# One transformer trunk layer on one core: the first modulation's weight slices issued by ScalarE, its vectors made as columns, and VectorE's order at the beginning and between the halves

## What is computed

```python
c_act = jax.nn.silu(c)
mod = (c_act @ w_ada[l] + b_ada[l])[:, None, :]
sh1, sc1, g1, sh2, sc2, g2 = jnp.split(mod, 6, axis=-1)
h = rms_norm(x, norm1_g[l]) * (1.0 + sc1) + sh1
proj = h @ w_in[l]          # attention q, k, v | conformer | short gated convolution | pooling
...
x = x + g1 * mix
h = rms_norm(x, norm2_g[l]) * (1.0 + sc2) + sh2
x = x + g2 * (jnp.square(jax.nn.relu(h @ w_ff1[l])) @ w_ff2[l])
```

## Time and profile before

| | |
|---|---|
| median of 3 runs | 2392.0 us (2390.57 to 2394.45) |
| the profiled execution | 2397.45 us |
| its span | 2395.2 us, mean granted clock of TensorE 0.978 |
| TensorE busy | 2304.6 us, 96% |
| VectorE busy | 1750.8 us, 73% |
| ScalarE busy | 983.4 us, 41% |
| GpSimd busy | 342.5 us, 14% |
| DMA | 177.67 MB, mean 74 GB/s |

### The profile page before, as it was taken

The page is one execution under the profiler, slowest core; times in us unless marked ns, Lnnn a source line. Parts: engine busy times, 40 slices in busy tenths (PEclk is TensorE's granted clock), DMA queues, the critical chain, the costliest instruction groups (busy, mean ns, idle before and its releaser), DMA issues.

```text
span 2395.2 us, 31303 instructions
## 1 busy us (share of the span) xinstructions
PE 2304.6 (96%) x11618; PEld 1943.3 (81%) x11618; DVE 1750.8 (73%) x2654; ACT 983.4 (41%) x1607; POOL 342.5 (14%) x245
## 2 busy tenths in 40 slices
PE   5999899987989999999999999999999999999999
PEld 3987897666888888888888888888888888888887
DVE  5548796888989786777676776767687676767676
ACT  4532555458888754423232323233433222223231
POOL 0343044822345440000000000000000000000000
PEclk9999999988999989999999999999999999999999
DMA  7441533120000034111111111136201111111112
GB/s 259 154 154 53 162 115 129 58 92 23 14 14 23 10 106 132 36 53 53 53 53 53 53 45 60 35 105 210 79 18 53 53 53 53 53 53 53 53 53 88
DMA packets 108278, 177.67 MB, mean 74 GB/s; under 512 B 5512, under 2 KB 77468, under 8 KB 107164
## 3 DMA queue, kind: packets, MB, share of 16 engines
q1 hardware_dynamic: 108188, 176.45, 22.3%
HBM read 152.84 MB, written 23.59 MB: 74 GB/s over the span
## 4 chain that ended last, share of the span: by engine, by line
PE 83%; DVE 9%; DMA 3%; ACT 3%; issue 2%; POOL 1%; SPq 1%; DVEq 0%; ACTq 0%; POOLq 0%
PE ps L2470 10%; PE ps L2468 10%; PE ps L2469 10%; PE ps L2506 7%; PE ps L2505 7%; PE ps L2507 7%; PE ps L2171 5%; PE ps L2172 5%; PE ps L2173 5%; PE ps L2358 3%; PE ps L2343 2%; PE ps L2413 2%; PE ps L2414 2%; PE ps L2415 2%; PE ps L2378 2%; DVE ps L1592 2%
## 5 line engine op out<-in xcount | busy, mean ns | idle before, releaser
L1958 DVE TENSOR_TENSOR sb_x_new<-sb_x_new,ps 128x512 f32<-128x512 f32 x512 | 347.3, 684 | 107.4 <-PE ps L2470 101.9
L2468 PE MATMUL ps<-sb_w_hi,sb_u_hi 128*128 128x512 f32 x1024 | 398.3, 389 | 0.0
L2469 PE MATMUL ps<-sb_w_lo,sb_u_hi 128*128 128x512 f32 x1024 | 398.3, 389 | 0.0
L2470 PE MATMUL ps<-sb_w_hi,sb_u_lo 128*128 128x512 f32 x1024 | 398.3, 389 | 0.0
L2470 PEld LDWEIGHTS ps<-sb_w_hi,sb_u_lo 128*128 128x128 f32 x1024 | 192.2, 188 | 39.9
L2468 PEld LDWEIGHTS ps<-sb_w_hi,sb_u_hi 128*128 128x128 f32 x1024 | 192.2, 188 | 39.9
L2469 PEld LDWEIGHTS ps<-sb_w_lo,sb_u_hi 128*128 128x128 f32 x1024 | 192.2, 188 | 39.9
L2173 PE MATMUL ps<-sb_h_hi,sb_w_lo 128*128 128x512 f32 x512 | 199.4, 389 | 0.0
L1405 ACT ACTIVATE ps<-ps 128x512 f32<-128x512 f32 x28 | 16.3, 582 | 410.7 <-PE ps L2507 410.7
L2171 PE MATMUL ps<-sb_h_hi,sb_w_hi 128*128 128x512 f32 x448 | 178.7, 399 | 0.7 <-DVE sb_w_lo L1919 0.7
L2172 PE MATMUL ps<-sb_h_lo,sb_w_hi 128*128 128x512 f32 x448 | 174.6, 390 | 0.0
(11 more groups left out here) (279 smaller groups left out, 4970.6 us busy)
## 6 DMA issues: line engine op xcount, KB each, us to landing
sb_w_full<-in_w_ff SPq DMA_DIRECT2D x34, 1024.0 KB, 5.0
sb_w_full<-in_w_ff SPq DMA_DIRECT2D x56, 512.0 KB, 3.7
sb_w_raw<-in_w_in SPq DMA_DIRECT2D x16, 1024.0 KB, 6.0
sb_ada<-in_w_ada SPq DMA_DIRECT2D x32, 512.0 KB, 5.3
sb_ada_first<-in_w_ada SPq DMA_DIRECT2D x8, 1024.0 KB, 14.2
sb_x_in<-in_x SPq DMA_DIRECT2D x16, 512.0 KB, 5.3
sb_mix_in<-mix_scratch SPq DMA_DIRECT2D x16, 512.0 KB, 5.0
sb_x_new<-in_x SPq DMA_DIRECT2D x16, 512.0 KB, 4.8
```

The lines of the kernel that those rows point to most:

```text
L1958: V.tensor_tensor(out=y, in0=y, in1=psum[:, 4 + p % 4, :], op=ALU.add).then_inc(ff2_read, 1)
L2468: M(dst, uh, wh[:, j, col], start=j == order[0], stop=False, skip_group_check=fast)
L2469: M(dst, uh, wl[:, j, col], start=False, stop=False, skip_group_check=fast)
L2470: ins = M(dst, ul, wh[:, j, col], start=False, stop=j == order[1], skip_group_check=fast)
```

## The change

Six edits:
1. SP no longer issues slices 0 to 3; ScalarE issues them as the first thing in its program. SP issues slices 4 to 7 with tile 0 of x ahead of slice 4 and tile 1 ahead of slice 6.
2. For the shift, TensorE takes the slice as the stationary side and `silu_c[:, k]` as one column: eight products by one column for each slice, into eight columns of bank 2. The shift stands there as a column; VectorE adds the bias straight from `psum`.
3. TensorE transposes tile 0 after slice 5.
4. `w_in_tail(0)` comes after the two vectors on VectorE.
5. `modulation(h, 0)` makes the norm vector by eight products by one column instead of two wide ones; `columns`, `diag_sum` and `diag_tmp` are gone.
6. Between the halves VectorE does `load_squares(10)`, `h_tail(8)` and `scale_rows(10)` ahead of three taps.

```diff
--- before.py
+++ after.py
@@ -61,6 +61,7 @@
 PLAIN = 2
 FAST = FG - PLAIN
 BROADCASTS = 7
+FROM_ACT = 4
 
 
 R_C, R_B, R_N1, R_N2 = 0, 8, 56, 64
@@ -217,7 +218,6 @@
         inv_first = sb("inv_first", 5.5, [P, GC, POOL_HALO])
         bn = sb("bn", 5.6875, [P, 2, 6])
         stat = sb("stat", 5.75, [P, 16])
-        diag_sum = sb("diag_sum", 5.8125, [P, 2 * DC])
         eps_col, lam_neg = small[:, 0:1], small[:, 1:2]
         gate_row = sb("gate_row", 6, [P, 2, D])
 
@@ -252,7 +252,6 @@
 
         ada_first = [sb(f"ada_first{k}", 14 + 8 * k, [P, 2 * D]) for k in range(DC)]
         ada_sum = sb("ada_sum", 171, [P, D])
-        diag_tmp = sb("diag_tmp", 175, [P, D])
         w_raw_first = [w_raw] + [sb(f"w_raw_first{w}", 118 + 8 * w, [P, ITEM]) for w in (1, 2)]
         table1 = sb("table1", 183, [R_END1, P])
         table2 = sb("table2", 183.5, [R_END2, P])
@@ -596,10 +595,10 @@
                 sp.dma_start(by_k8(w_raw_in(w)), w_in_v[:, :, c0:c0 + GW]).then_inc(w_in_loaded(w)[0], 16)
 
             sp.dma_start(lam_in[:, :, :], lam_params[0, :, :].partition_broadcast(P)).then_inc(lam_ld, 16)
-            for k in range(DC):
+            for k in range(FROM_ACT, DC):
+                if k in (4, 6):
+                    sp.dma_start(x_in[k // 2 - 2][:, :], x_v[:, k // 2 - 2, :]).then_inc(x_ld[k // 2 - 2], 16)
                 sp.dma_start(ada_first[k][:, :], w_ada_v[:, k, 0:2 * D]).then_inc(ada0_ld[k], 16)
-                if k in (3, 5):
-                    sp.dma_start(x_in[k // 2 - 1][:, :], x_v[:, k // 2 - 1, :]).then_inc(x_ld[k // 2 - 1], 16)
             load_w_in(0)
             load_w_in(1)
             load_small()
@@ -999,6 +998,8 @@
                 A(h_hi[:, :, t * P:(t + 1) * P], tmp[:, :, :], ACT.Copy).then_inc(hhi_ready, 1)
 
 
+            for k in range(FROM_ACT):
+                act.dma_start(ada_first[k][:, :], w_ada_v[:, k, 0:2 * D]).then_inc(ada0_ld[k], 16)
             act.wait_ge(const_ready, 1)
             A(ident_r[:, :], ident[:, :], ACT.Copy)
             A(mask_r[:, :], h_tmp[:, 0, :], ACT.Copy).then_inc(act_chain, 1)
@@ -1490,15 +1491,6 @@
                 V.tensor_tensor(out=w_lo[w % 3][:, :], in0=w_raw_in(w), in1=f32(w_hi[w % 3][:, :]),
                                 op=ALU.subtract).then_inc(wlo_ready, 1)
 
-            def columns(rows, n, tmp):
-
-
-                blocks = tmp.rearrange("p (m c) -> p m c", c=P)
-                link(V.tensor_tensor(out=blocks, in0=rows.rearrange("p a n -> p (a n)").rearrange("p (m c) -> p m c", c=P),
-                                     in1=ident[:, :].rearrange("p (o c) -> p o c", o=1).to_broadcast([P, n, P]), op=ALU.mult))
-                link(V.tensor_reduce(out=diag_sum[:, 0:n], in_=blocks, axis=AX.X, op=ALU.add))
-
-
             groups = [(cc, slice(64 * s, 64 * s + 64), 2 << (2 * cc + s)) for cc in range(GC) for s in range(2)]
             for cc, part, win in groups:
                 V.memset(inv_win[part, cc:cc + 1], 1.0 / win)
@@ -1539,15 +1531,14 @@
                 normalise(n, x_in[n][:, :], x_in[n][:, :])
             add_slice(6)
             add_slice(7)
-            w_in_tail(0)
             dve.wait_ge(mod1_mm, 1)
-            columns(psum[:, 2:4, :], DC, diag_tmp[:, :])
-            V.tensor_tensor(out=shift1[:, :], in0=diag_sum[:, 0:DC], in1=col1[:, R_B:R_B + 8], op=ALU.add)
+            V.tensor_tensor(out=shift1[:, :], in0=psum[:, 2, 0:DC], in1=col1[:, R_B:R_B + 8], op=ALU.add)
             dve.wait_ge(mod1_mm, 2)
             link(V.scalar_tensor_tensor(out=gain1[:, :], in0=psum[:, 4, 0:DC], scalar=float(GW), in1=col1[:, R_B + 8:R_B + 16],
                                         op0=ALU.mult, op1=ALU.add))
             V.scalar_tensor_tensor(out=gain1[:, :], in0=gain1[:, :], scalar=1.0, in1=col1[:, R_N1:R_N2],
                                    op0=ALU.add, op1=ALU.mult).then_inc(mod1_ready, 1)
+            w_in_tail(0)
             V.memset(conf[:, :, 0:TAPS - 1], 0.0)
             V.memset(ud[:, :, 0:POOL_HALO], 0.0)
             link(V.memset(halo2[:, :, :], 0.0))
@@ -1668,9 +1659,8 @@
 
             def read_norm_vector(h):
                 dve.wait_ge(mod2_mm, 2 * h + 1)
-                columns(psum[:, 6:8, :], DC, h_tmp[:, :, :].rearrange("p k t -> p (k t)"))
                 r = R_B + (3 + h) * DC
-                vector = V.scalar_tensor_tensor(out=(gain2 if h else shift2)[:, :], in0=diag_sum[:, 0:DC], scalar=float(GW),
+                vector = V.scalar_tensor_tensor(out=(gain2 if h else shift2)[:, :], in0=psum[:, 6, 0:DC], scalar=float(GW),
                                                 in1=col1[:, r:r + DC], op0=ALU.mult, op1=ALU.add)
                 if h:
                     link(vector)
@@ -1767,16 +1757,16 @@
                     short(h, cc, b)
                     if h == 0 and cc == b == 0:
                         w_in_tail(NI + 1)
+                    if h == 0 and (cc, b) == (GC - 1, 0):
+                        load_squares(HT + 2)
+                        h_tail(HT, h_tmp)
+                        scale_rows(HT + 2)
                     if h or b == 0:
                         pump(taps, 3)
                     if h and (cc, b) == (GC - 1, 0):
                         ln_scale(1, 0)
-                    if h == 0 and (cc, b) == (GC - 1, 0):
-                        h_tail(HT, h_tmp)
-                        load_squares(HT + 2)
                     if h == 0 and (cc, b) == (0, 1):
                         h_tail(HT + 1, h_tmp)
-                        scale_rows(HT + 2)
                 if h == 0:
                     link(V.tensor_copy(halo2[:, :, :], prod[:, :, HALF:HALF + STAPS - 1]))
 
@@ -2189,12 +2179,12 @@
             pe.wait_ge(siluc_ready, 1)
             for k in range(DC):
                 pe.wait_ge(ada0_ld[k], 16)
-                for m in range(2):
-                    ins = M(psum[:, 2 + m, :], silu_c[:, k:k + 1].to_broadcast([P, P]), ada_first[k][:, m * BLK:(m + 1) * BLK],
-                            start=(k == 0), stop=(k == DC - 1), skip_group_check=True)
+                for m in range(DC):
+                    ins = M(psum[:, 2, m:m + 1], ada_first[k][:, m * P:(m + 1) * P], silu_c[:, k:k + 1],
+                            start=(k == m == 0), stop=(k == DC - 1), skip_group_check=True)
+                if k == 5:
+                    transposes(0, x_in[0])
             ins.then_inc(mod1_mm, 1)
-            pe.wait_ge(tab_col, 2)
-            transposes(0, x_in[0])
             pe.wait_ge(mod1_sum, DC)
             for k in range(DC):
                 ins = M(psum[:, 4, k:k + 1], ada_sum[:, k * P:(k + 1) * P], ones_mean[:, 0:1], start=True, stop=True)
@@ -2240,8 +2230,12 @@
                     pe.wait_ge(norm_read, h + 1)
                 else:
                     pe.wait_ge(ada_used, (h + 1) * DC)
-                for n in range(2):
-                    ins = M(psum[:, 6 + n, :], ones_mean[:, :], mod_sums(h)[1 - s][:, n * BLK:(n + 1) * BLK], start=True, stop=True)
+                if s:
+                    for n in range(2):
+                        ins = M(psum[:, 6 + n, :], ones_mean[:, :], mod_sums(h)[0][:, n * BLK:(n + 1) * BLK], start=True, stop=True)
+                else:
+                    for k in range(DC):
+                        ins = M(psum[:, 6, k:k + 1], mod_sums(h)[1][:, k * P:(k + 1) * P], ones_mean[:, 0:1], start=True, stop=True)
                 ins.then_inc(mod2_mm, 1)
 
             def ln_sum(h, b, s):
```

## The result

| | before | after |
|---|---|---|
| median, same chip | 2390.6 us (20 runs, 2387.8 to 2394.5) | 2394.4 us (20 runs, 2391.9 to 2401.0) |
| ratio, 95% interval | | 1.0018 [1.0012, 1.0025] |
| the profiled execution | 2397.45 us | 2392.43 us |
| its span | 2395.2 us | 2390.3 us |

The account below looks back on a forecast made before the run. TensorE, busy for 96% of the span, was taken to bound the kernel. Start -0.5, between the halves -1.6, second half -2.4 and -1.5 summed to -6.0, put on 2392.0: forecast 2386 us, range 2379.5 to 2391.5.

Parts of the forecast that it names:

- the one costed at nothing: Start: ScalarE's four slice issues (2.06) end near 4.8, before it is first needed at 6.70; cost nothing.
- rival 2: Start gives back what the rest wins: +0.8, up to +2 with late tables; 2389, no change; 0.21 together with rival 4.
- bound A: Start, two DMA queues: served in order of issue, fourth slice there at 15.3, first modulation at 38.5.
- bound B: Start, two DMA queues: equal shares, fourth slice there at 21.5, first modulation at 41.3.
- column group: Start, TensorE: 16 one-column rows for a slice at 1.2 GHz, put at 2.9, nine groups in all.
- Start in all: Start: first modulation at 41.0 instead of 41.7, less 0.2 for TensorE's clock; -0.5.
- between the halves: Tile 10's wait of 5.26 goes, but the third weight's low half bounds the half; only -1.6 stays.
- the second half's -2.4: Second half's norm vector: VectorE's products come earlier, the 1.10 wait goes, 3.42 becomes about 2.2; -2.4.
- clock term: End of second half's projections: with less waiting TensorE's clock may hold; -1.5 (0 to -3).
- Rival 3: Start: one-column rows pay 0.33 per weight load, +14 to +18, modulation later than 52, about 2402; chance 0.06.
- Rival 1: Start: the clock rises during the modulation, groups cost 1.9, middle -6.5; 2380 in all; chance 0.13.
- Rival 4: Between the halves: x of tile 10 isn't there at 256.6, costing that term; 0.21 together with rival 2.

Follow-up runs that it names:

- o5: Kernel before with only the norm vectors of both halves made as columns: 2387.4 us, ratio 0.9985.
- o6: Kernel before with only statistics, low half and scaling of tile 10 put ahead of three taps: 2390.7 us, ratio 1.0001.
- w1: Kernel after with two wide products of each slice added beside the eight columns, their result not read: 2404.8 us, ratio 1.0051.
- u1: Kernel after with all eight slices issued by SP again, the columns on TensorE kept: 2388.5 us, ratio 0.9993.
- t2: Kernel after with ScalarE issuing slice 0 alone and SP the other seven: 2388.1 us, ratio 0.9985.
- w2: u1 with five 512-column products on TensorE ahead of the modulation as a warm-up, their result not read: 2387.4 us, ratio 0.9984.
- o4: Kernel before with only the low half of the first projection weight moved after the two vectors: 2387.0 us, ratio 0.9981.

## Why the prediction was wrong, point by point

**The step that failed** is the one costed at nothing: "ScalarE is first asked for something at 6.70, when the transposed tables are there", and with it "TensorE works without a break from about 10 (slice 0 and silu are there by then)". The issue itself was as written (2.06 for four, the copies by 4.64). What was left out is that the tables, on SP's queue, now run beside 4 MB on another one. The text spoke of both queues for slices 3 to 7 only. They landed at 14.67 instead of about 6, TensorE began at 17.45, and undoing the issue gave back 5.3 (not the whole 7.45 to the forecast's 10, since with SP's issue slice 0 lands only at 12.0). "Up to +2 if the tables come late" stood in rival 2 and was too small by more than half.

**The rule that was cited spoke to this.** From 9 to 12 us the trace shows 113 packets against 111 with thirteen times the bytes. The Trainium skill ("DMA: Bandwidth & Descriptors", "Queues, rings and completion order") says that an engine takes turns between its queues a packet at a time; the trace agrees from 9 to 12 us, while from 4 to 9 the packets were 282 to 140. I had turned it into equal shares of bytes. With packets of some 500 bytes ahead on SP's queue, ScalarE got nearly all the bytes: its 4.19 MB had been moved by 15 us, and SP's queue had moved 0.52. That is bound A's 15.3, not bound B's 21.5. So B was wrong for the slices and the omission wrong for the tables, for the same reason.

**The mis-sized term** is the column group. That the clock would stay at 1.2 GHz was right. Its price was put at 2.9, with the argument that only the load doubles, not the streaming; it was 3.42 (from start to start 20.5 for six and 6.7 for two, then 3.55 for the gain's), nearly twice the 1.87. The whole row scales with the clock. And TensorE never waited for a slice, so all nine groups are on the path: 17.45 + 9 x 3.42 + 1.74 for the transposes + 0.44 of hand-offs = 50.4. With the forecast's own start of 10 and 2.9 it would have been bound A's 38.5: the late tables added 7.4 to that, the price 4.6. That the forecast was 41.0 and not 38.5 is luck: its 2.5 more came from slices that were not late.

**Start in all:** forecast -0.5, measured +8.7 (the modulation at 50.37, beyond the 43 that the prediction named as its sign of being wrong), and another +1.0 by tile 9, since TensorE comes to its projections at the low clock and the rise comes 4.2 behind the first one (59.96), against 2.1 before (49.2).

**Right:** the weight's landing (forecast 30.8, its copy started at 31.06); `columns` and `w_in_tail(0)` off the path (4.7 forecast; edit 4 alone gave 5.1); nothing from the first half's norm vector (tile 9 at 256.35 against 256.11 in o5); between the halves -1.6 forecast with the third weight as bound, -2.0 measured in the kernel after and in o6, tile 11's wait of about 2.5 with it (2.56 and 2.67); the second half's -2.4 and the last wait of "about 2.2" (2.05). Its clock term, -1.5 of 0 to -3, was -3.3 in the kernel after and -1.6 in o5: from the first pool product to the end of the projections before took 36.77, after 31.05 and o5 32.72, and 2.5 of each difference are the waits. It is a spread and not a size. Up to the end of the projections the stretches of the two profiles are 8.7 + 1.0 - 2.0 - 5.7 = +2.0 (504.45 - 502.50). The medians say +3.8; where the other 1.8 lie is open, since profiles are single executions.

**Slips in its sums.** "TensorE's slice 7 is done at 38.9 in B" counts the gain's group; by its own terms slice 7 ends at 21.5 + 5 x 2.9 + 1.6 = 37.6. Nothing hangs on it. The range's upper edge, 2391.5, follows from no sum: rival 2 with its +2 ends at 2390.0, or at 2390.8 if the 2 comes on top of its 0.8. And the terms were put on the median of three runs, 2392.0, where twenty gave 2390.6; the difference is what the terms forecast, -6.0, and it came out at +3.8.

**The rivals.** What happened lies between rivals 2 and 3: the start gave back more than the rest won, through the tables and a price between 3.1 and 5.3 for a group. Rival 3's condition, a modulation later than 52, was nearly met at 50.4. Rival 1 (the clock rises) is out by the rows themselves: a group cost 3.42 to the end of the modulation, where w1 shows 1.84 at the high clock. Rival 4 is out: VectorE began tile 10's statistics at 265.96 without a wait. The forecast gave a loss of at most 2 at the start a weight of 0.21 and one of 14 to 18 a weight of 0.06, and nothing to the 8.7 between; it should have priced the start from the landing of the last small transfer.

## What to carry to other kernels

Before large transfers move to a second queue, list the small ones on the first queue that something waits for: here they took turns with the large ones packet by packet, and their delay grew with the bytes on the other queue, not with their own. Put one large transfer there, or move the small ones. A matrix-vector product turned into one-column rows looks as cheap as the wide one at the full clock, but in after, u1 and t2 it paid the price of the low clock throughout, and in w2 from its first 2 us on: price it so, and measure it. And read gains of a few us from landmarks that lie ahead of the part that varies from run to run, and from medians of many runs; here the two profiles as totals had the wrong sign.

## What the runs showed of the hardware that I had not expected

- From 9 to 12 us two queues shared packets one to one (113 to 111) and bytes 13 to 1; from 4 to 9 packets two to one (282 to 140). A table issued at 4.36 landed at 14.67 with 4 MB on the other queue; with 1 MB there the same table, issued at 3.77, landed at 7.44, and with nothing there TensorE had it by 6.18 (before).
- One-column rows of f32 cost 0.213 each (3.41 for 16) at 1.2 GHz and 0.115 (1.84) at 2.4 GHz; the ratio is 1.85, nearly the clock's. The wide ones: 3.76 and 1.96 for four.
- TensorE and its weight loads, busy almost without a break for some 30 us with one-column rows and a few transposes, stayed at the price of 1.2 GHz in after, u1, t2 and w2, in w2 from the first 2 us on, though they began there at 2.4 GHz.
- A kernel that mixes both kinds of rows (w1) has two times, 2393.5 to 2397.2 and 2412.4 to 2414.1, where o4, o5 and o6 beside it spread over 5 to 6.
